# Residual sum and layer-norm statistics taken one PSUM bank at a time in a hybrid decoder layer

## What is computed

```
h = hybrid_token_mixer(x, w_in, ...)            # GLA + MoBA branches, gates, @ w_out
x = layer_norm(2**0.25 * x + h, ln1_g, ln1_b)
h = peer_ffn(x, w_q, sub_keys, u_tab, v_tab)    # product-key routing over 128*128 experts
x = layer_norm(2**0.25 * x + h, ln2_g, ln2_b)

layer_norm: mu = mean(x), var = mean((x-mu)^2);  (x-mu) * rsqrt(var + 1e-5) * g + b
```

## Time and profile before

| | |
|---|---|
| three runs, median | 1135.03 us |
| profiled execution, first to last instruction (span) | 1132.8 us |
| PE busy | 1091.1 us (96%) |
| DVE / ACT / POOL busy | 815.5 / 555.7 / 589.1 us |

### The profile page before, as it was taken

One profiled execution on the slowest core, in us unless ns is written; L12 is line 12 of the kernel. 1 busy time (PEld: TensorE's weight loads), 2 busy tenths in 40 slices (PEclk: granted clock), 3 DMA queues, 4 the chain that ended last, 5 costly groups with the idle time before them and its releaser, 6 DMA issues.

```text
span 1132.8 us, 20715 instructions
## 1 busy us (share of the span) xinstructions
PE 1091.1 (96%) x6734; PEld 966.9 (85%) x6734; DVE 815.5 (72%) x1398; ACT 555.7 (49%) x898; POOL 589.1 (52%) x452
## 2 busy tenths in 40 slices
PE   6999999986999999999989999999999999999995
PEld 4887887675999999999989999997888888888884
DVE  4347656365899988888997888976666666666666
ACT  4347544542345555455555555554444444444442
POOL 5484345443322346666556667655555555555554
PEclk9999999997999999999999999999999999999998
DMA  6655344342545554444434444446555555555552
GB/s 200 240 187 167 130 161 137 111 149 77 166 157 182 169 180 154 162 151 165 157 124 164 149 132 146 134 161 216 192 186 185 185 186 187 187 190 193 186 186 93
DMA packets 52474, 186.51 MB, mean 165 GB/s; under 512 B 6209, under 2 KB 6593, under 8 KB 52433
## 3 DMA queue, kind: packets, MB, share of 16 engines
q1 hardware_dynamic: 51584, 182.87, 48.5%
q0 software_dynamic: 848, 3.15, 0.8%
HBM read 184.94 MB, written 1.05 MB: 164 GB/s over the span
## 4 chain that ended last, share of the span: by engine, by line
PE 84%; DVE 8%; DMA 3%; issue 2%; POOL 2%; ACT 1%; DVEq 0%; SPq 0%; POOLq 0%
PE ps L1150 15%; PE ps L1151 15%; PE ps L1152 15%; PE ps L1450 10%; PE ps L1452 10%; PE ps L1451 10%; PE ps L1410 5%; DVE wlo L717 2%; DMA raw<-w_tiles_in 1%; POOL wlo L346 1%; PE ps L1190 1%; DVE hot L1024 1%; ACT whi L482 1%; DVE sel L1029 1%; PE ps L1377 1%
## 5 line engine op out<-in xcount | busy, mean ns | idle before, releaser
L346 POOL TENSOR_TENSOR wlo<-raw,whi 128x256 fp32r<-128x256 f32 x341 | 440.2, 1292 | 497.7 <-ACT whi L482 497.2
L717 DVE TENSOR_TENSOR wlo<-raw,whi 128x768 fp32r<-128x768 f32 x341 | 361.4, 1060 | 254.5 <-ACT whi L482 253.0
L482 ACT ACTIVATE whi<-raw 128x1024 fp32r<-128x1024 f32 x344 | 364.2, 1059 | 331.4 <-DMA raw<-w_tiles_v 180.4
L1150 PE MATMUL ps<-ahi,whi 128*128 128x256 f32 x1152 | 333.5, 290 | 3.0 <-DVE wlo L717 1.6
L1151 PE MATMUL ps<-alo,whi 128*128 128x256 f32 x1152 | 326.4, 283 | 0.0
L1152 PE MATMUL ps<-ahi,wlo 128*128 128x256 f32 x1152 | 326.2, 283 | 0.0
L1150 PEld LDWEIGHTS ps<-ahi,whi 128*128 128x128 f32 x1152 | 221.4, 192 | 3.8 <-DVE wlo L717 2.0
L1151 PEld LDWEIGHTS ps<-alo,whi 128*128 128x128 f32 x1152 | 221.7, 192 | 0.0
L1152 PEld LDWEIGHTS ps<-ahi,wlo 128*128 128x128 f32 x1152 | 221.2, 192 | 0.0
L1450 PE MATMUL ps<-whi,hhi 128*128 128x512 f32 x512 | 202.4, 395 | 1.1 <-POOL wlo L346 1.1
L1451 PE MATMUL ps<-wlo,hhi 128*128 128x512 f32 x512 | 202.2, 395 | 0.0
(11 more groups left out here) (190 smaller groups left out, 998.3 us busy)
## 6 DMA issues: line engine op xcount, KB each, us to landing
raw<-w_tiles_u SPq DMA_DIRECT2D x128, 512.0 KB, 3.3
raw<-w_tiles_v SPq DMA_DIRECT2D x128, 512.0 KB, 3.3
raw<-w_tiles_in SPq DMA_DIRECT2D x64, 512.0 KB, 3.3
raw<-w_tiles_q SPq DMA_DIRECT2D x16, 512.0 KB, 3.4
raw<-w_tiles_out SPq DMA_DIRECT2D x8, 512.0 KB, 3.3
xraw<-xT SPq DMA_DIRECT2D x4, 256.0 KB, 6.3
xt<-x POOLq DMA_DIRECT2D x1, 1024.0 KB, 5.6
out<-xt SPq DMA_DIRECT2D x4, 256.0 KB, 2.0
```

What stands on the lines that cost most here:

```text
L346: pool.tensor_tensor(wlo[:, tile.slot, DVE_COLS:], raw[:, tile.slot, DVE_COLS:], whi[:, tile.slot, DVE_COLS:].bitcast(F32), ALU.subtract)\
L482: act.activation(whi[:, tile.slot, :], raw[:, tile.slot, :], ACT.Copy)\
L717: dve.tensor_tensor(wlo[:, tile.slot, 0:DVE_COLS], raw[:, tile.slot, 0:DVE_COLS], whi[:, tile.slot, 0:DVE_COLS].bitcast(F32), ALU.subtract)\
L1150: pe.matmul(out, ah, bh, start=start, stop=False)
```

## The change

In both stages the tail now runs bank by bank: the loop over the two column halves is outside the loop over the three tiles, and a semaphore `bank_done` (in place of `half_done`) is raised after each of the first three banks. A tile raises `tiles_used` in the last bank only. DVE's `total` takes one bank, with a wait between sum and `bn_stats`. Half 1's first bank is taken before half 0's reciprocal and shift; half 0's product with g (first norm) moves behind all of half 1's statistics, `x1_low(0)` behind `apply(1)`, and `apply` finishes one column half before it starts the other.

```
-            def total(t):
-                for half in range(2):
-                    xs = xt[:, t, half * CW:(half + 1) * CW]
-                    own.step(... sum ...)
-                own.wait()
-                for half in range(2):
-                    own.step(dve.bn_stats(...))
-                own.wait()
+            def total(t, half):
+                if t == 0 or half == 0:
+                    dve.wait_ge(S["bank_done"], 3 * n + 2 * t + half + 1)
+                else:
+                    dve.wait_ge(S["tiles_used"], tiles)
+                own.do(... sum of this bank ...)
+                own.step(dve.bn_stats(stats[:, t, half, :], xs))
+            def variance(t):
+                own.wait()
                 own.do(dve.bn_aggr(...))
...
-                for cols in halves:
-                    own.step(... (x - mean) * g ...)
-                own.wait()
-                for cols in halves:
+                for half in range(2):
+                    own.do(... (x - mean) * g ...)
                     ... x * rstd + b ... .then_inc(S[done], 1)
-            dve.wait_ge(S["half_done"], n + 1)
-            total(0)
+            total(0, 0)
+            total(0, 1)
+            variance(0)
+            total(1, 0)
             ... wait ln_sqrt, reciprocal, shift of half 0 ...
+            total(1, 1)
+            variance(1)
             if n == 0:
+                dve.sem_inc(S["lo_ready_dve"], AHEAD)
                 dve.wait_ge(S["ln_scaled"], 1)
                 dve.tensor_tensor(xt[:, 0, :], xt[:, 0, :], g, ALU.mult).then_inc(S["ln_times_g"], 1)
-            dve.wait_ge(S["tiles_used"], tiles)
-            if n == 0:
-                dve.sem_inc(S["lo_ready_dve"], AHEAD)
-            total(1)
+            apply(1)
             if n == 0:
                 x1_low(0)
-            apply(1)
...
         for t in range(NT):
-            for k in range(TILES_OUT - TAIL, TILES_OUT):
-                ...
-                last = out_half(tile, k, t)
-                if t == 1:
-                    last.then_inc(S["tiles_used"], 1)
-            if t == 0:
-                last.then_inc(S["half_done"], 1)
+            for half in range(2):
+                for k in range(TILES_OUT - TAIL, TILES_OUT):
+                    ...
+                    last = out_half(tile, k, t, (half,))
+                    if t == 1 and half == 1:
+                        last.then_inc(S["tiles_used"], 1)
+                if t == 0 or half == 0:
+                    last.then_inc(S["bank_done"], 1)
```

More of the change, by code:

```diff
@@ L294, in layer @@
              "ln_shift ln_scaled ln_times_g ln_sqrt ln_done x1_tp ln_done0 out_ready0 q_copied sc_done "
-             "sc_copied hid_used r_neg r_exp half_done sel_done sel_tp selT_done iotas_ready hot_ready "
+             "sc_copied hid_used r_neg r_exp bank_done sel_done sel_tp selT_done iotas_ready hot_ready "
              "hot_i_ready hot_j_ready g_done g_used merged w_hi w_lo out_ready stored dve_own "
@@ L911, in layer_norm @@
         def layer_norm(banks, n, g, b, tiles, done):
-            def total(t):
-                for half in range(2):
-                    xs = xt[:, t, half * CW:(half + 1) * CW]
-                    own.step(dve.scalar_tensor_tensor(out=xs, in0=xs, scalar=ALPHA, in1=ps[:, banks[2 * t + half], :],
-                                                      op0=ALU.mult, op1=ALU.add))
-                own.wait()
-                for half in range(2):
-                    own.step(dve.bn_stats(stats[:, t, half, :], xt[:, t, half * CW:(half + 1) * CW]))
+            def total(t, half):
[3 more added lines that the diff above has]
+                    dve.wait_ge(S["tiles_used"], tiles)
+                xs = xt[:, t, half * CW:(half + 1) * CW]
+                own.do(dve.scalar_tensor_tensor(out=xs, in0=xs, scalar=ALPHA, in1=ps[:, banks[2 * t + half], :],
+                                                op0=ALU.mult, op1=ALU.add))
+                own.step(dve.bn_stats(stats[:, t, half, :], xs))
+            def variance(t):
                 own.wait()
@@ L930, in apply @@
                 own.do(dve.reciprocal(rstd[:, t:t + 1], rstd[:, t:t + 1]))
-                halves = [slice(half * CW, (half + 1) * CW) for half in range(2)]
-                for cols in halves:
-                    own.step(dve.scalar_tensor_tensor(out=xt[:, t, cols], in0=xt[:, t, cols], scalar=mv[:, t, 0:1],
-                                                      in1=g[:, cols], op0=ALU.subtract, op1=ALU.mult))
-                own.wait()
-                for cols in halves:
+                for half in range(2):
+                    cols = slice(half * CW, (half + 1) * CW)
+                    own.do(dve.scalar_tensor_tensor(out=xt[:, t, cols], in0=xt[:, t, cols], scalar=mv[:, t, 0:1],
+                                                    in1=g[:, cols], op0=ALU.subtract, op1=ALU.mult))
                     dve.scalar_tensor_tensor(out=xt[:, t, cols], in0=xt[:, t, cols], scalar=rstd[:, t:t + 1],
                                              in1=b[:, cols], op0=ALU.mult, op1=ALU.add).then_inc(S[done], 1)
-            dve.wait_ge(S["half_done"], n + 1)
-            total(0)
+            total(0, 0)
+            total(0, 1)
+            variance(0)
+            total(1, 0)
             dve.wait_ge(S["ln_sqrt"], NT * n + 1)
@@ L1320, in _, with out_half @@
         turn_y(0)
-        def out_half(tile, k, t):
-            for half in range(2):
+        def out_half(tile, k, t, halves=(0, 1)):
+            for half in halves:
                 cols = slice(half * CW, (half + 1) * CW)
@@ L1338, in _ @@
         for t in range(NT):
-            for k in range(TILES_OUT - TAIL, TILES_OUT):
-                tile = Tile(T_OUT + k)
-                tile_ready(tile)
-                last = out_half(tile, k, t)
-                if t == 1:
-                    last.then_inc(S["tiles_used"], 1)
-            if t == 0:
-                last.then_inc(S["half_done"], 1)
+            for half in range(2):
+                for k in range(TILES_OUT - TAIL, TILES_OUT):
+                    tile = Tile(T_OUT + k)
+                    tile_ready(tile)
+                    last = out_half(tile, k, t, (half,))
[3 more added lines that the diff above has]
+                    last.then_inc(S["bank_done"], 1)
         for t in range(NT):
@@ L1441, in _, with values @@
         hidden(after(CHUNKS - 1) + 1, TILES_U)
-        def values(tile, t, start, stop):
+        def values(tile, t, start, stop, halves=(0, 1)):
             tok = slice(t * P, (t + 1) * P)
-            for half in range(2):
+            for half in halves:
                 cols = slice(half * CW, (half + 1) * CW)
@@ L1476, in _ @@
         for t in range(NT):
[L1477 to L1483, removed]
+            for half in range(2):
+                for m in range(T_END - TAIL, T_END):
+                    values_ready(Tile(m))
+                    last = values(Tile(m), t, False, m == T_END - 1, (half,))
+                    if t == 1 and half == 1:
+                        last.then_inc(S["tiles_used"], 1)
+                if t == 0 or half == 0:
+                    last.then_inc(S["bank_done"], 1)
     block.__exit__(None, None, None)
```

## The result

The changed kernel takes 1139.59 us, median of six executions (1138.43 to 1143.44), beside 1135.18 for the kernel before: ratio 1.0045, 95% interval 1.0033 to 1.0057, so 5.1 us slower (3.7 to 6.5). The medians alone lie 4.4 us apart; all differences to the kernel before are taken from the ratios. The forecast was 2.9 us: right in sign, and too small.

A forecast was written before the change was run, and what follows sets the result against it. PE holds 84% of the chain of waits, with DVE setting the end after it; first norm 1.7 plus end 1.2 made 2.9 us, span 1135.7, 1137.9 us in all; range 1136.9 to 1138.9, with rivals 1135.2 to 1139.6.

The forecast's parts named there:

- The sign: Whole kernel: slower, by 2.9 us; chances slower 0.61, same 0.32, faster 0.07.
- the two mechanisms: Both norms: matmul cover lost before the late tile, 1.40 us, and POOL, 1.47 us later at the end, meeting more DVE products.
- What PE loses: Both tails: PE reaches the late tile after 6 matmuls, not 12, stands 2.2 us at the value tile, loses 1.40 us.
- the third: Rival, after the norm: longer idle holds PE's low clock about as long again, giving 1139.4 us; chance 0.12.
- Lost cover: Both norms: 6 matmuls of 0.233 us no longer stand ahead of the late tile's wait, 1.40 us each.
- Second norm, +1.2: Kernel's end: DVE's last product ends at 1131.54 us, not 1130.37, so 1.2 us later.
- POOL and VectorE in turn: Kernel's end: instructions with both inputs in SBUF alternate; the first product ends 0.54 us behind POOL's multiply.
- Rival 2: Both norms: DVE goes first whenever both wait; first norm -2.6 us, end +2.9, total 1135.3 us; chance 0.10.
- First norm, +1.7: First norm: the query projection starts near 275.9 us, 1.7 us later; both full splits stand among DVE's products.
- a clause for that case: First norm: if half 1's square root comes later, the first split wins and the end is 0.25 us later.
- An added wait costs 0.12 us: DVE's sum and statistics: neighbours start 0.60 us apart, with a wait between 0.72, so 0.12 us more in half 0.
- Rival 1: Both norms: late tiles arrive 2.1 us sooner or PE was slowed elsewhere, cover not lost; about 1135.0 us; chance 0.10.

The follow-up runs named there:

- e8: The changed kernel itself, unaltered, measured a second time: ratio 1.0054 to the kernel before.
- e1: The kernel before with only TensorE's new bank-by-bank order in both tails, VectorE's old order kept: ratio 1.0034 to the kernel before.
- e3: The changed kernel with eight further matmuls, into an unread bank, in TensorE's pause before the last value tile: ratio 1.0035 to the kernel before.
- e9: The changed kernel with eight further matmuls in the pause before the last value tile, timed again: ratio 1.0039 to the kernel before.
- e10: The changed kernel with further matmuls filling TensorE's pauses in both tails, into an unread bank: ratio 1.0029 to the kernel before.
- e11: The changed kernel without GpSimd's three instructions in the second norm, so its output is incomplete: ratio 1.0006 to the kernel before.
- e7: The changed kernel with token half 0 tile by tile, half 1 bank by bank, and VectorE's and ScalarE's queues reordered: ratio 0.9982 to the kernel before.

## Why the prediction was wrong

The sign, and the two mechanisms that it summed, held. The term that failed is in "What PE loses": "Loss: 6 x 0.233 = 1.40 us. It can't be more (the tile is fixed)". It can: behind the pause, which the prediction itself put at 2.2 us, the clock often fell, and the 30 matmuls then took up to 1.6 us longer. At the two tails it fell in nine of fourteen open pauses of 1.5 us and more. The prediction priced the pause as if the clock held through it, as it had through 0.76 us. The range ended at 1139.6, and 1.0045 times 1135.03 is 1140.1; the median, 1139.59, touches that end.

The clock did stand among the rivals, as the third, but at another place: behind the norm, where it was low before as well, and was to stay low about twice as long. There it stayed for 4.4 us from the start of the projection (274.24) where it had stayed for 3.7 (from 274.18), a cost of about 0.35 us; the rows show the windows in which it rose, of the kernel before, then of the changed one:

```profile
277.00:278.00 1.00, 1.00 (x7) 1.00 (x7) 0.00 (x0) 0.00 (x0) 0.00 (x0) 0.57 0.00 0
...
278.00:279.00 1.00, 1.00 (x8) 1.00 (x7) 0.00 (x0) 0.00 (x0) 0.00 (x0) 0.68 0.00 0
```

In e8, the same kernel, it was 3.3 us. That this rival's 1139.4 lies near the median is luck.

Step by step:

- Lost cover, 1.40 in each norm: 1.36 and 1.39 in e1, where the clock held. Right as the cost of the cover.
- Second norm, +1.2: +1.01 where the clock held (e3, e8, e9, e10). Right, with the shift 1.36 us later against the tile (1125.62 - 1118.94 in e3, 1121.43 - 1116.11 before) where 1.47 were put.
- POOL and VectorE in turn: the first product ends 0.55 us behind POOL's multiply, 0.54 were put, and e11 shows the cause. Rival 2, in which VectorE goes first, occurs in no trace.
- First norm, +1.7: +1.76 (changed) and +1.74 (e10). The sum was right, one step in it was not: the square root was done 13.5 us behind the tile instead of 12.3, since the load came later (12.4 us behind the tile, not 11.0), and the first product met a split where a bias was expected. The prediction had a clause for that case, 0.25 us more.
- An added wait costs 0.12 us: sum to statistic 0.72 apart in all traces (1119.07 - 1118.35 in the changed kernel), neighbours without a wait 0.60. The Trainium skill (VectorE: DVE Perf Modes, The DRAIN you can't avoid) found a semaphore after each of eight `tensor_copy` to cost nothing extra; these traces, of other instructions, do not agree.
- Rival 1, that the cover isn't lost, is out by e1 and by the pauses. One reading against it was not right: in the first norm the kernel before waited 0.62 us ahead of the last output tile but one (251.96), and stood for none at the last (253.52).

Open: what decides whether the clock falls behind a given pause; and three long executions (1143.4 and 1144.4 us of the changed kernel, 1146.0 of e9) with mean clocks of 0.984 to 0.986, of which no profile exists.

## What to carry to other kernels

Finishing an accumulation bank by bank brings the last tile's wait forward: count the matmuls that stood ahead of that wait, and price the longer pause twice, once as lost cover and once, as a risk, as matmuls at half clock behind it. Only reorder the part whose tiles are all there. Before moving work between engines, look for instructions of VectorE with two SBUF inputs that stand beside GpSimd's: here they ran in turn, and a GpSimd instruction that nobody waits for soon belongs behind them. That brought 4.1 us here, twice what the whole reordering of e7 did.

## What the hardware showed that was not expected

The granted clock fell behind eight pauses of TensorE of 1.7 to 2.1 us, and once behind one of 1.30 after 0.53, although TensorE was busy up to them; it held behind five of 1.5 to 2.2 us (one of them 1.00 and 0.81 together). Where it fell, 1.2 GHz lasted for 7 or 8 matmuls of 512 columns at 0.43 us each. In the four pauses that were filled with matmuls into a bank nobody reads it never fell, at no cost in the two stretches. VectorE's four products take 0.75 us each when left alone, and up to 2.83 in turn with GpSimd.
